# Spatial gating's gates: three passes of rounded parts and remainders in place of full 32-bit products

## The reference

```python
u, v = split(gelu(h @ w_in), 2)                         # w_in: 1024 x 4096, u and v: 256 x 2048
v = rms_norm(v.reshape(b, n, 128, 8, 256), v_norm)      # over each group of 256 columns
w_causal = where(tril, w_s, 0)                          # 8 groups of 128 x 128
gate = einsum('gij,bnjgc->bnigc', w_causal, v) + b_s.T[:, :, None]
return (u * gate.reshape(b, s, 2048)) @ w_out
```

## Time and profile before

| | us |
|---|---|
| median of three runs | 1071.15 |
| the profiled execution | 1071.83 |
| its span | 1070.0 |
| TensorE busy in the span | 1049.0 |
| VectorE busy | 813.6 |
| ScalarE busy | 564.1 |

### The profile page before, as it was taken

The page is one execution under the profiler, slowest core; times in us unless marked ns, Lnnn a source line. Parts: engine busy times, 40 slices in busy tenths (PEclk is TensorE's granted clock), DMA queues, the critical chain, the costliest instruction groups (busy, mean ns, idle before and its releaser), DMA issues.

```text
span 1070.0 us, 19233 instructions
## 1 busy us (share of the span) xinstructions
PE 1049.0 (98%) x8325; PEld 961.9 (90%) x8325; DVE 813.6 (76%) x1071; ACT 564.1 (53%) x695; POOL 46.4 (4%) x32
## 2 busy tenths in 40 slices
PE   8999999999789999999999999999999999999998
PEld 8999987898678899999789999878888889999986
DVE  5876789899853686768988777898665647766797
ACT  6644446585764554445655444565665436444451
POOL 1000000110162000000000000000000000000000
PEclk9999999999999999999999999999999999999999
DMA  9755556563000665565546655566655456565551
GB/s 308 232 188 171 193 197 187 165 197 119 1 4 18 222 197 178 179 196 194 199 158 197 196 170 186 198 199 223 191 169 182 166 156 213 176 196 176 180 195 40
DMA packets 127214, 184.91 MB, mean 173 GB/s; under 512 B 4221, under 2 KB 101738, under 8 KB 127002
## 3 DMA queue, kind: packets, MB, share of 16 engines
q1 hardware_dynamic: 126384, 181.85, 52.6%
q0 software_dynamic: 448, 1.71, 0.5%
q10 hardware_dynamic: 298, 0.12, 0.0%
HBM read 182.62 MB, written 1.05 MB: 172 GB/s over the span
## 4 chain that ended last, share of the span: by engine, by line
PE 80%; DVE 14%; issue 4%; ACT 2%; ACTq 0%; DVEq 0%
PE banks L1514 22%; PE banks L1516 22%; PE banks L1515 22%; DVE wlo L958 3%; DVE arena L1030 2%; DVE rounded L1038 2%; PE banks L1957 2%; DVE raw L1032 1%; DVE arena L1031 1%; PE banks L1676 1%; PE banks L1677 1%; PE banks L1675 1%; DVE wlo L1040 1%; PE banks L1592 1%; PE banks L1593 1%
## 5 line engine op out<-in xcount | busy, mean ns | idle before, releaser
L950 DVE TENSOR_TENSOR wlo<-raw,whi 128x2048 fp32r<-128x2048 f32 (+1 forms) x142 | 322.4, 2281 | 106.5 <-ACT whi L498 106.4
L1514 PE MATMUL banks<-xTh,whi 128*128 128x256 f32 x1392 | 394.6, 283 | 2.0 <-DVE wlo L1173 1.8
L498 ACT ACTIVATE whi<-raw 128x2048 fp32r<-128x2048 f32 (+1 forms) x170 | 311.0, 1842 | 160.2 <-PE banks L1516 143.5
L1516 PE MATMUL banks<-xTh,wlo 128*128 128x256 f32 x1392 | 393.9, 283 | 0.0
L1515 PE MATMUL banks<-xTl,whi 128*128 128x256 f32 x1392 | 393.9, 283 | 0.0
L1514 PEld LDWEIGHTS banks<-xTh,whi 128*128 128x128 f32 x1392 | 267.2, 192 | 3.0 <-issue 2.5
L1515 PEld LDWEIGHTS banks<-xTl,whi 128*128 128x128 f32 x1392 | 267.2, 192 | 0.0
L1516 PEld LDWEIGHTS banks<-xTh,wlo 128*128 128x128 f32 x1392 | 267.2, 192 | 0.0
L1514 PE MATMUL banks<-whi,hTh 128*128 128x512 f32 (+1 forms) x192 | 77.8, 405 | 1.3 <-DVE wlo L1040 1.0
L1516 PE MATMUL banks<-whi,hTl 128*128 128x512 f32 (+1 forms) x192 | 74.7, 389 | 0.0
L1515 PE MATMUL banks<-wlo,hTh 128*128 128x512 f32 (+1 forms) x192 | 74.6, 388 | 0.0
(11 more groups left out here) (289 smaller groups left out, 1529.9 us busy)
## 6 DMA issues: line engine op xcount, KB each, us to landing
raw<-in_ffn_w_down SPq DMA_DIRECT2D x44, 1024.0 KB, 4.9
raw<-in_ffn_w_gate SPq DMA_DIRECT2D x43, 1024.0 KB, 5.4
raw<-in_ffn_w_up SPq DMA_DIRECT2D x43, 1024.0 KB, 5.4
raw<-in_sg_w_in SPq DMA_DIRECT2D x16, 1024.0 KB, 5.5
raw<-in_ab_w_in SPq DMA_DIRECT2D x8, 1024.0 KB, 5.1
raw<-in_sg_w_out SPq DMA_DIRECT2D x8, 1024.0 KB, 4.9
raw<-in_ab_w_out SPq DMA_DIRECT2D x4, 1024.0 KB, 5.0
raw<-in_ab_w_in SPq DMA_DIRECT2D x2, 832.0 KB, 4.4
```

What stands on the lines that cost most here:

```text
L498: A(whi[:, j % SLOTS, 0:n], raw[:, j % RAW_SLOTS, 0:n], ACT.Copy).then_inc(S("hi_ready"), 1)
L950: TT(wlo[:, j % RAW_SLOTS, 0:n], raw[:, j % RAW_SLOTS, 0:n], whi[:, j % SLOTS, 0:n].bitcast(f32), ALU.subtract).then_inc(S("lo_ready"), 1)
L1514: mm(out_ap, lh, rh, start=first, stop=False)
L1516: return mm(out_ap, ll, rh, start=False, stop=last)
```

## The change

The transposed gating weights and the normalized v are each split in a rounded part and a remainder, and the 16 products of the gates become `split_mm`, three passes each. wsT is replaced by wsTh and wsTl, in parts of hTh and hTl that this stage leaves free; Vh lies in the rounded region at N0, and Vl over V itself. ScalarE copies V's chunk to Vh after the two `hi`, once VectorE's scaling is done, and counts it in `v_gelu`, which so goes by three per chunk. VectorE forms Vl = V - Vh between the two `lo`, counted in `v_ready` (five per chunk). In chunk 0, after the second `lo`, VectorE forms wsTl for the two halves out of banks 6 and 7, and `wsT_ready` goes to 4. The waits are renumbered to match.

```diff
@@ -237,8 +237,9 @@
         T_AT = [N0, XT0 + 1536]
         T_SUM, T_HI, T_LO = [at(o, 1536) for o in T_AT], [at_r(o, 1536) for o in (N0 + 1536, XT0)], [at_r(o, 1536) for o in T_AT]
         V1, V2, V34 = at(XT0 + 3072, 512), at(XT0 + 3584, 512), at(N0, 2, 512)
-        wsT = at(4096, GROUPS, P)
+        wsTh, wsTl = (a[:, 16:20, :].rearrange("p k (o n) -> p (k o) n", n=P) for a in (hTh, hTl))
         V = at(R0 + 4096, NT, SGW)
+        Vh, Vl = (at_r(o, NT * SGW).rearrange("p (t n) -> p t n", n=SGW) for o in (N0, R0 + 4096))
         v_norm_row = at(R0 + 2048, SGW)
         ws_raw = at(0, GROUPS, P)
 
@@ -873,25 +874,27 @@
                     A(V[:, t, 512 * c:512 * c + 512], B[2 * (c % 2) + t][:], ACT.Gelu, scale=rstd[:, t:t + 1]
                       ).then_inc(S("v_gelu"), 1)
                 if c:
-                    act.wait_ge(S("v_ready"), 4 * c)
-                act.wait_ge(S("v_gelu"), 2 * c + 2)
+                    act.wait_ge(S("v_ready"), 5 * c)
+                act.wait_ge(S("v_gelu"), 3 * c + 2)
                 for t in range(NT):
                     for g in range(2):
                         A(squares[t][:, CG * g:CG * g + CG], V[:, t, 512 * c + CG * g:512 * c + CG * g + CG],
                           ACT.Square, accum_out=v_ss[:, 2 * t + g:2 * t + g + 1]).then_inc(S("v_squared"), 1)
                 hi(b + 2 * c + 4)
                 hi(b + 2 * c + 5)
+                act.wait_ge(S("v_ready"), 5 * c + 4)
+                A(Vh[:, :, 512 * c:512 * c + 512], V[:, :, 512 * c:512 * c + 512], ACT.Copy).then_inc(S("v_gelu"), 1)
                 if c == 0:
                     for n in range(2):
                         act.wait_ge(S("wsT_sums"), n + 1)
-                        A(wsT[:, 4 * n:4 * n + 4, :], B[6 + n][:].rearrange("p (g n) -> p g n", n=P), ACT.Copy
+                        A(wsTh[:, 4 * n:4 * n + 4, :], B[6 + n][:].rearrange("p (g n) -> p g n", n=P), ACT.Copy
                           ).then_inc(S("wsT_ready"), 1)
                 else:
                     gate_out(c - 1)
             for c in range(4):
                 act.wait_ge(S("unit_done"), b + 8 + 2 * c + 2)
                 if c == 0:
-                    act.wait_ge(S("v_ready"), 16)
+                    act.wait_ge(S("v_ready"), 20)
                 else:
                     act.wait_ge(S("y_ready"), c)
                 for t in range(NT):
@@ -1486,7 +1489,16 @@
                         STT(V[:, t, cols], V[:, t, cols], v_ss[:, 2 * t + g:2 * t + g + 1], v_norm_row[:, cols],
                             ALU.mult, ALU.mult).then_inc(S("v_ready"), 1)
                 lo(b + 2 * c + 4)
+                cols = slice(512 * c, 512 * c + 512)
+                dve.wait_ge(S("v_gelu"), 3 * c + 3)
+                dve.wait_ge(S("v_ready"), 5 * c + 4)
+                TT(Vl[:, :, cols], V[:, :, cols], Vh[:, :, cols].bitcast(f32), ALU.subtract).then_inc(S("v_ready"), 1)
                 lo(b + 2 * c + 5)
+                if c == 0:
+                    for n in range(2):
+                        dve.wait_ge(S("wsT_ready"), 2 * n + 1)
+                        TT(wsTl[:, 4 * n:4 * n + 4, :], B[6 + n][:].rearrange("p (g n) -> p g n", n=P),
+                           wsTh[:, 4 * n:4 * n + 4, :].bitcast(f32), ALU.subtract).then_inc(S("wsT_ready"), 1)
             for c in range(4):
                 dve.wait_ge(S("u_gelu"), 2 * c + 2)
                 dve.wait_ge(S("gate_ready"), 4 * c + 4)
@@ -2170,21 +2182,22 @@
 
             def gates(c):
 
-                pe.wait_ge(S("v_ready"), 4 * c + 4)
+                pe.wait_ge(S("v_ready"), 5 * c + 5)
                 if c:
                     pe.wait_ge(S("gate_ready"), 4 * c)
                 else:
-                    pe.wait_ge(S("wsT_ready"), 2)
+                    pe.wait_ge(S("wsT_ready"), 4)
                 for t in range(NT):
                     for g in (2 * c, 2 * c + 1):
-                        last = mm(B[6 + t][:, CG * (g % 2):CG * (g % 2) + CG], wsT[:, g, :],
-                                  V[:, t, CG * g:CG * g + CG], start=True, stop=True)
+                        cols = slice(CG * g, CG * g + CG)
+                        last = split_mm(B[6 + t][:, CG * (g % 2):CG * (g % 2) + CG], wsTh[:, g, :], wsTl[:, g, :],
+                                        Vh[:, t, cols], Vl[:, t, cols], True, True)
                     last.then_inc(S("gate_sums"), 1)
 
             for c in range(8):
                 for u in range(2):
                     if c >= 2 and u == 0:
-                        pe.wait_ge(S("v_gelu"), min(2 * (c - 1), 8))
+                        pe.wait_ge(S("v_gelu"), 3 * min(c - 2, 3) + 2)
                         if c >= 6:
                             pe.wait_ge(S("u_gelu"), 2 * (c - 5))
                     gemm(b + 2 * c + u, (2 * (c % 2), 2 * (c % 2) + 1), 4 * u, KD, XS, 4 if c == 0 else None)
```

## The result

The changed kernel takes 1073.39 us, the median of 22 runs from 1070.99 to 1075.99, against 1071.42 us for the kernel before (22 runs, 1069.82 to 1074.68). The ratio is 1.0017 with a 95% interval of 1.0010 to 1.0025: slower by 1.1 to 2.7 us, under the 0.3% that count here. The forecast was 1.6 us more, 1072.8 us.

What follows compares the result with a forecast made beforehand. TensorE, busy 98%, bounds the kernel: chunk 0's group ends 2.47 us later, groups 1 to 3 save 0.87, so 1.6 us more on the median 1071.15 gives 1072.8 us; own range 1071.5 to 1074.0, wider range 1070.0 to 1075.6.

Steps and rivals of the forecast that it cites:

- The stall: Chunk 0: TensorE stands from 761.45 to 764.0 us for wsTl in VectorE's queue; its first group ends 2.47 us later.
- The groups: Four groups of gate products, one per chunk: twelve passes take 1.44 us instead of 1.73, saving 0.29 us each.
- The hidden work: ScalarE's added 4.2 us and VectorE's 6.3 us lie beside TensorE's work, all but chunk 0's wait.
- the margins: Chunks 1 to 3: no new wait; in chunks 2 and 3 Vl is ready 1.5 us before TensorE asks.
- A: Chunk 0: no stall, the weights' remainders are ready; 1.16 us saved, 1070.0 us; chance 0.08.
- C: Groups of chunks 2 and 3 wait for Vl too; 1 us too late gives 1074.8 us; chance 0.07.
- Rival B: TensorE loses its clock in chunk 0's stall, returning at 1.2 GHz; 1.4 to 6.9 us added; chance 0.11.

Runs made afterwards that it cites:

- e2: Changed kernel with the wsTl subtractions moved ahead of unit b+5's remainder in VectorE's queue; stage 50.71 us, ratio to the kernel before 0.9992.
- e1: Changed kernel with wsTh ahead of Vh on ScalarE, wsTl and Vl ahead of both units' remainders on VectorE; ratio to the kernel before 0.9989.
- e6: Changed kernel with weights first in both queues and full 32-bit products of the rounded parts, so added work only; ratio to the kernel before 1.0001.
- e4: Changed kernel with Vl moved behind both units' remainders in all four chunks; stage 55.35 us, 3.96 more than the kernel before, one run.
- e3: Changed kernel with full 32-bit products of the rounded parts, remainders formed but not used; ratio to the kernel before 1.0033.
- e10, e7, e9, e12: The changed kernel itself profiled again, nothing changed; clock fell behind the stall, stage 54.46 to 54.49 us.

## Why the prediction was right, and where not

**The stall: right.** VectorE's queue was to end 14.3 us after the first Gelu (764.0 less 749.71) and ended after 14.2 (761.71 less 747.48). Group 0 was to be over 2.47 us later than before. Taken to the second pass behind the group, it is 13.53 us after the first Gelu before (763.24) and 16.10 after (763.58): 2.57 us. e2 shows that the place of wsTl in that queue makes 2.3 us of the stall; with e1's order, which also puts ScalarE's copies of the weights ahead of Vh, nothing of it is left.

**The groups: right, a little better.** Four times 0.29 us was worked out from 0.12 us a pass; the passes came 0.118 us apart, and four times 0.32 us was gained (e1), 0.95 us of it in groups 1 to 3 of the changed kernel where 0.87 was forecast. That the sum comes out at 1.62 us where 1.6 was forecast is in part luck: 0.10 us too little of stall and 0.08 us too little of gain cancel. The shorter distance of 109 ns, an estimate by the Trainium skill (TensorE: Matmul & The Clock Gate, "Back-to-back issue gap"), was not reached.

**The hidden work and the margins: right.** e6 puts the price of the added work at 0.00 us; chunks 1 to 3 had no wait, and e4 delayed Vl by 2.2 us in each, and that opened a wait of 0.6 us in chunk 2 alone, so the margin there was 1.6 us where 1.5 was worked out. Rivals A and C are out for the changed kernel.

**Rival B: its weight was wrong.** It got 0.11, against evidence that did not carry: one profile in which a wait had not cost the clock. The wait at 272 to 274 us, moreover, is the one of 1.7 us (L1988 behind L746); the longest one, of 2.2 us, lies at 278 to 281 us, so the prediction joined two waits:

```profile
280.69 1.08 PE L1911 MATMUL banks<-arena,C 64*64 64x512 f32 x4 [2.24 <-ACT small L776]
280.00:286.00 6.00, 4.10 (x31) 3.18 (x32) 5.53 (x12) 4.69 (x16) 0.00 (x0) 1.00 0.00 0
```

The wait of 2.2 us did keep the clock, here and in all eight profiles that show it at that length. But behind the shorter one, of 1.7 us, the clock did fall in other executions, as in e1's profile:

```profile
272.00:274.00 2.00, 0.44 (x4) 0.45 (x5) 1.90 (x7) 2.00 (x8) 0.00 (x0) 1.00 0.00 0
274.00:276.00 2.00, 2.00 (x11) 1.55 (x12) 1.69 (x10) 2.00 (x5) 0.00 (x0) 0.54 0.00 0
```

B happened in 4 of 7 profiled executions of the changed kernel. Its price, 1.5 us, came out near the lower end given (1.4 us for group 0 alone), but not in the way told there: TensorE did not come back at 1.2 GHz. In these four the group's first passes ran at the upper level, the clock fell within the group's first microsecond, and it stayed low for about 3 us, into the passes over 512 columns. With a fall the kernel is 3.1 us slower, at the edge of what counts, and without one 1.6. With 4 in 7 the mean would be 2.4 us (three at 1.5 to 1.6, four at 3.1); the runs' 1.1 to 2.7 us hold that and the forecast's 1.6 alike. That the time lies in the forecast's own range, 1071.5 to 1074.0, is therefore in part luck: the forecast counted on a clock that fell in more than half of these profiles, and it was the low price of a fall that kept the time inside.

The mean granted clock that stands on record for each run says more than the times. In the profiles one fall anywhere leaves a mean of 0.998 (e1, e2, e3, e10), two leave 0.996 or 0.997 (e7, e9, e12). Of the 22 runs of the changed kernel 12 stand at 0.997 or below, with a mean time of 1074.2 us against 1072.4 of the other ten; of the 38 runs of the kernel before for which the experiments recorded a clock, 4 do. These means cannot place a fall, but the difference fits a stall that often costs the clock better than the 0.11 that B was given. The warning of the Trainium skill, that idle time between bursts of matmuls costs the full clock (TensorE: Matmul & The Clock Gate, "Why this matters for your kernels"), agrees with these traces in part of the executions: behind the stall in five of nine profiles, behind the wait of 2.2 us in none of eight. What decides in which was not found.

## What to carry to other kernels

When a change hands an engine more work in order to shorten another's, place the new instructions by when their results are asked for: here the remainder of unit b+5, which TensorE asks for only 24 passes (5.4 us) behind the first group, stood ahead of one that the group itself asks for, and turned 1.3 us of gain to 1.6 us of loss with the clock kept. Follow the in-order queue instruction by instruction with durations of the same shape, and the stall comes out to a tenth of a microsecond. Count a stall of TensorE of some microseconds as its length and a chance of a slower clock behind it, and don't infer from a single profile that the clock will stay.

## What was not expected of the hardware

The same program with the same stall, of 2.5 to 2.6 us, keeps TensorE's upper clock in some executions and loses it in others: it fell in four of the seven profiles of the changed kernel, and in five of nine with those of e3 and e4, which have the same stall. Behind the wait of 1.7 us in the attention part it fell in six of the fourteen profiles, and not always in the same ones: e10 and e12 lost it at the stall and kept it there. A third place lies near 310 us, behind a wait that the profile puts down to issue: there it fell in the three profiles in which that wait took 1.5 to 1.7 us (e2, e4, e12), and in none of the others, where it took at most 1.2. The wait at 278 us kept the clock each time that it took 2.2 us, so the length of a wait alone does not decide. With its first Gelu at 747.0 to 750.2 us in these profiles the stage also starts up to 3.2 us earlier or later with nothing changed ahead of it, which is more than the change moves; stretches between fixed instructions repeat to about 0.1 us.
